# A hybrid language model's step: the second layer's recurrence from chunks of 32 to chunks of 64 tokens, with two preparations interleaved

## The chip, the core and the metric

The kernel runs on one core of a Trainium2 chip. TensorE (PE) multiplies, VectorE (DVE) and ScalarE (ACT) work on its results, GpSimd (POOL) does a few element-wise products and starts some DMAs, SyncE (SP) starts the weight loads. The metric is the device time of one execution in microseconds, the median of several runs.

## The reference

One forward step of a two-layer model with width 1024 over 512 prompt tokens and 8 decode sequences of 4 tokens (T = 544 columns). Layer 0 mixes tokens with two gated linear recurrences, layer 1 with the recurrence of RWKV-7; each is followed by a feed-forward part and a gated embedding part. The change is in layer 1's recurrence, which the reference runs token by token, for 16 heads of 64:

```python
def step(s, inp):
    r_t, lw_t, k_t, v_t, kk_t, a_t = inp
    s_kk = jnp.einsum('bhik,bhk->bhi', s, kk_t)
    s = (s * jnp.exp(lw_t)[:, :, None, :]
         - s_kk[..., :, None] * (kk_t * a_t)[..., None, :]
         + v_t[..., :, None] * k_t[..., None, :])
    return s, jnp.einsum('bhij,bhj->bhi', s, r_t)
```

The kernel computes it in chunks: within a chunk the tokens' mutual effect is a triangular system, whose inverse turns the removals and the values into updates; between chunks only the 64 x 64 state of each head is handed on.

## The kernel before, in words

All activations lie transposed, features on partitions and tokens on columns. Weights are split into an fp32r head and a rest (`w_head`, L293 on ACT; `w_rest`, L298 on DVE), and `unit_products` (L329) makes the dense products of all layers out of three fp32r products. `mixed` (L1742) and `dve_x` (L1751) make the inputs of layer 1's four projections r, k, g1 and v on DVE.

In layer 1, `dve_mix` scans the log decays per chunk (resets from `scan_resets(CO)`, CO = 32), `act_r` stores r, `act_k` and `dve_k` turn k, the decays and the removal keys into four scaled operands per feature tile: two key operands (`kb`, by chunk) and two query operands (`qrF`, `qr`). `wc` keeps the decay at each chunk's end.

The recurrence stands in `odd_late`. Four quads of 128 tokens and a fifth for the decode batch are prepared by `pe_prepare`, `act_prepare` and `dve_prepare`, which are generators: each `go_on(preparation, n)` lets an engine do the next n parts. The parts of a quad, in `parts_of`, are:

- sc: the key-query products of its 4 chunks (L2056), masked by DVE (L2159) and moved by ACT (L2133) and DVE (L2135),
- P and X for levels 2 to 5: the inverse is built by doubling. A level takes 128 P instructions (L2074), a copy by ACT (L2119), 128 X instructions (L2080), then on DVE a subtraction (L2179), a block transposition (L2197) and a masked product (L2198). Blocks are 32 x 32,
- vt and kt: transposes of values (L2066) and keys (L2069) to token rows, copied by ACT (L2111, L2115) or DVE (L2175).

A part's results go to one of PSUM banks 7, 0 and 1, and a part waits for the reader of its bank. A chunk n (`pe_chunk`, `act_chunks_odd`, `dve_chunks_odd`) has six streams of 16 products each on PE (32 instructions, since every fp32 product is two): av (L2217), R against the state (L2232), the state's part of the outputs oR (L2241), U through the inverse (L2247), and the two closing products, outputs (L2257) and new state (L2263). Between them stand ACT's copies of R (L2273) and half of U (L2277), DVE's other half of U (L2295), then DVE adds the state (h, L2303) and decays it (H, L2308), and ACT stores the outputs (L2285). The order on each engine is fixed: the quad's next parts are issued after R/oR (two), after U (one) and after the closing products (two). Each engine runs its own queue in order, so what stands in the queue behind a wait waits too.

The states of the decode sequences are loaded by GpSimd's DMA queue into two slots (`pool_states`, L2319), transposed by PE (L2086), stored by ACT (L2121) or DVE (L2184), and read for the decode tokens (L2094). `pool_masked_values` (L2353) makes masked values on GpSimd. `pe_late` (L2415) begins the gate part.

## Time and profile before

| | us |
|---|---|
| median of 3 runs | 2081.32 (2080.29 to 2083.05) |
| profiled execution | 2076.66 |
| its span | 2074.9 |
| PE busy | 1834.3 (88%) |
| DVE busy | 1026.3 (49%) |
| ACT busy | 720.8 (35%) |
| GpSimd busy | 128.7 (6%) |
| mean PE clock granted, share of full speed | 0.898 |

A row of a busy-time view has the stretch's start and end, its length, then for each engine the busy time and the number of instructions, then the PE clock as a share of full speed (0.50 is 1.2 GHz, 1.00 is 2.4 GHz), the DMA engines' mean share and GB/s. A timeline row has start, duration, engine, line, operation, output, input, shape and count, and in brackets the idle time before it and who ended it. A row of merged instructions lasts until the last one's modelled end, which overlaps the next row a little. In the chain of waits "issue" is time in which an engine waits for nothing that the profile shows. PEld is PE's weight load.

### The profile page before, as it was taken

How to read it: one execution, taken by the hardware profiler on the slowest of the kernel's cores; microseconds unless marked ns; L12 is line 12 of the kernel's file. 1: busy time of each engine (PE TensorE's matmuls, PEld its weight loads, DVE VectorE, ACT ScalarE, POOL GpSimd, SP SyncE). 2: the span in 40 equal slices, each digit the busy share in tenths (PEclk: the TensorE clock that was granted, in tenths of full speed). 3: DMA queues.
4: the chain of work that ended last, by engine and by line, in shares of the span. 5: the costliest groups of instructions: out<-in, count | busy, mean ns of one | idle time of the engine just before them, and what ended most of it. 6: DMA issues, size and time to landing. Idle time of an engine off the chain costs nothing.

```text
span 2074.9 us, 47908 instructions
## 1 busy us (share of the span) xinstructions
PE 1834.3 (88%) x21171; PEld 1708.4 (82%) x21171; DVE 1026.3 (49%) x1438; ACT 720.8 (35%) x923; POOL 128.7 (6%) x152
## 2 busy tenths in 40 slices
PE   4999977999999999957989767768889999999996
PEld 3999874999999999936868666657379999999996
DVE  5377766544334444566685433322464443444443
ACT  3353355254322224223453121211435451222333
POOL 1032450000000000000000000000100000000000
PEclk8999988999999999978999766665699999999998
DMA  3321131433322232211212100010024333233321
GB/s 100 81 72 52 52 103 29 112 113 91 101 72 81 81 105 69 72 42 31 82 54 71 33 4 4 4 23 25 0 65 124 88 91 94 61 91 91 92 72 43
DMA packets 237101, 138.61 MB, mean 67 GB/s; under 512 B 6560, under 2 KB 232160, under 8 KB 236944
## 3 DMA queue, kind: packets, MB, share of 16 engines
q1 hardware_dynamic: 226528, 114.31, 19.0%
q0 software_dynamic: 4048, 13.67, 2.7%
q10 hardware_dynamic: 6368, 8.24, 1.2%
q8 instruction: 135, 2.21, 0.4%
q14 instruction: 22, 0.18, 0.0%
HBM read 128.04 MB, written 8.16 MB: 66 GB/s over the span
## 4 chain that ended last, share of the span: by engine, by line
PE 76%; DVE 13%; ACT 4%; issue 4%; POOL 1%; DMA 1%; ACTq 0%; DVEq 0%; POOLq 0%
PE ps L329 59%; PE ps L2080 2%; PE ps L2074 1%; PE ps L1498 1%; DVE w_rest L298 1%; PE ps L1700 1%; ACT w_head L293 1%; PE ps L2232 1%; DVE x_split L1751 1%; PE ps L2241 1%; PE ps L2056 1%; POOL mix L855 1%; PE ps L964 1%; PE ps L2257 1%; PE ps L2217 1%
## 5 line engine op out<-in xcount | busy, mean ns | idle before, releaser
L329 PE MATMUL ps<-x_split,w_head 128*128 128x272 f32 (+1 forms) x5568 | 946.3, 293 | 51.5 <-DVE x_split L1751 20.8
L329 PEld LDWEIGHTS ps<-x_split,w_head 128*128 128x128 f32 x5568 | 801.5, 192 | 72.2 <-issue 48.4
L329 PE MATMUL ps<-x_split,w_rest 128*128 128x272 f32 (+1 forms) x2784 | 582.8, 291 | 0.0
L329 PEld LDWEIGHTS ps<-x_split,w_rest 128*128 128x128 f32 x2784 | 442.7, 192 | 0.0
L293 ACT ACTIVATE w_head<-w_raw 128x1024 fp32r<-128x1024 f32 (+1 forms) x206 | 228.3, 1108 | 605.5 <-PE ps L329 595.1
L298 DVE TENSOR_TENSOR w_rest<-w_raw,w_head 128x1024 fp32r<-128x1024 f32 (+1 forms) x206 | 268.3, 1303 | 193.2 <-ACT w_head L293 193.1
L329 PE MATMUL ps<-hidden_split,w_head 128*128 128x272 f32 x1408 | 233.2, 287 | 0.0
L329 PEld LDWEIGHTS ps<-hidden_split,w_head 128*128 128x128 f32 x1408 | 198.0, 188 | 0.0
L329 PE MATMUL ps<-hidden_split,w_rest 128*128 128x272 f32 x704 | 145.3, 287 | 0.0
L329 PEld LDWEIGHTS ps<-hidden_split,w_rest 128*128 128x128 f32 x704 | 110.1, 188 | 0.0
L1330 DVE TENSOR_TENSOR hT<-hT,ps 128x544 f32<-128x544 f32 (+1 forms) x40 | 28.8, 721 | 161.1 <-PE ps L329 161.1
L1462 DVE TENSOR_TENSOR mix<-mix,ps 128x544 f32<-128x544 f32 x44 | 31.7, 721 | 126.7 <-PE ps L329 126.7
L1458 DVE TENSOR_TENSOR mix<-mix,ps 128x544 f32<-128x544 f32 x44 | 31.7, 721 | 64.7 <-PE ps L329 58.7
L1448 ACT ACTIVATE hidden_split<-mix 128x544 f32 (+1 forms) x44 | 29.0, 659 | 91.3 <-DVE mix L1466 91.3
L1468 DVE TENSOR_TENSOR hidden_split<-mix,hidden_split 128x544 f32 (+1 forms) x44 | 31.9, 725 | 42.5 <-ACT hidden_split L1448 42.5
L2074 PE MATMUL ps<-odd_quad 32*32 32x32 f32 x2080 | 31.4, 227 | 16.2 <-issue 8.2
L2074 PEld LDWEIGHTS ps<-odd_quad 32*32 32x32 f32 x2080 | 28.5, 140 | 20.3 <-issue 10.6
L293 ACT ACT_TABLE_LOAD x21 | 26.9, 1283 | 52.1 <-PE ps L329 40.6
L964 PE MATMUL ps<-mix 64*64 64x64 f32 (+1 forms) x896 | 36.6, 229 | 8.1 <-DVE mix L882 8.1
L855 POOL TENSOR_TENSOR mix<-mix 128x256 f32<-128x256 f32 (+1 forms) x36 | 32.3, 897 | 158.5 <-DVE mix L882 88.6
L964 PEld LDWEIGHTS ps<-mix 64*64 64x64 f32 (+1 forms) x896 | 30.8, 140 | 11.6 <-DVE mix L882 9.2
L504 DVE TENSOR_TENSOR mix<-mix 128x544 f32<-128x544 f32 x48 | 34.5, 719 | 4.1 <-ACT mix L498 4.1
(390 smaller groups left out, 1993.3 us busy)
## 6 DMA issues: line engine op xcount, KB each, us to landing
w_raw<-in_w_ffn_gate SPq DMA_DIRECT2D x44, 512.0 KB, 3.8
w_raw<-in_w_ffn_up SPq DMA_DIRECT2D x44, 512.0 KB, 3.8
w_raw<-in_w_ffn_down SPq DMA_DIRECT2D x32, 704.0 KB, 4.6
w_raw<-in_w_in_even SPq DMA_DIRECT2D x29, 512.0 KB, 3.8
w_raw<-in_w_ple_gate SPq DMA_DIRECT2D x16, 512.0 KB, 4.0
w_raw<-in_w_out_even SPq DMA_DIRECT2D x8, 512.0 KB, 4.0
w_raw<-in_rw_wr SPq DMA_DIRECT2D x8, 512.0 KB, 4.1
w_raw<-in_rw_wk SPq DMA_DIRECT2D x8, 512.0 KB, 3.9
```

What stands on the lines that cost most here:

```text
L293: act.activation(wh[:, s, 0:kt * P], raw[:, s, 0:kt * P], ACT.Copy).then_inc(head_ok[s], 1)
L298: dve.tensor_tensor(wl[:, s, 0:kt * P], raw[:, s, 0:kt * P], wh[:, s, 0:kt * P].bitcast(F32), ALU.subtract).then_inc(rest_ok[s], 1)
L329: mm = pe.matmul(ps[:, 2 * s + h, 0:half.stop - half.start], w[:, s, k * P:(k + 1) * P], x[:, k, half], start=first and k == 0, stop=k == ...
L504: dve.tensor_tensor(n.sum, n.sum, n.sq[:, s, :], ALU.add).then_inc(sum_ok, 1)
L855: pool.tensor_tensor(e[:, :, 0, :], mid, b[:, :, 0, :], ALU.subtract)
L964: mm = pe.matmul(ps[64 * (c % 2):64 * (c % 2) + CE, b0 + level // 2, at:at + CE], left[:, c * CE:(c + 1) * CE], right[:, c * CE:(c + 1) * CE],
L1448: act.activation(hid[:, 0, ds(j, 1), :], prod.unsqueeze(1), ACT.Copy).then_inc(hhead_ok, 1)
L1458: dve.tensor_tensor(two(act_out), two(norm_f.rs), out2(0), ALU.mult).then_inc(bank_free[0], 1)
L1462: dve.tensor_tensor(two(prod), two(norm_f.rs), out2(1), ALU.mult).then_inc(bank_free[1], 1)
L1468: dve.tensor_tensor(hid[:, 1, ds(j, 1), :], prod.unsqueeze(1), hid[:, 0, ds(j, 1), :].bitcast(F32), ALU.subtract).then_inc(hrest_ok, 1)
L2074: mm = pe.matmul(at_block(out, p, g, j, i), at_block(bT, p, g, j, i), at_block(xx, p, g, j, i), start=True, stop=True)
L2080: mm = pe.matmul(at_block(out, p, g, j, i), at_block(pp, p, g, j, i), at_block(xTs[q % 2], p, g, j, i), start=True, stop=True)
```

## The change

The prompt's recurrence runs in 8 chunks of 64 tokens (CP) in place of 16 of 32; the decode batch keeps its blocks of 32.

- Scaling. Decays are still scanned per 32 tokens. `dve_r` now takes each chunk's sum over its first half (`half{t}`) and subtracts it from both log operands of that half (`mid{t}`), so that each 64-token chunk is scaled about its middle. `act_k` takes the exponent of these sums, `dve_k` multiplies them into the chunks' end decays (`decays`); the last key product and the copy of the first are each split into prompt and decode.
- Blocks. The 16 heads lie on the four 64 x 64 quarters of the array (`tile_heads`). A chunk has its own preparation stream m: aT (scores for the inverse), P and X for levels 2 to 6, A (scores for values), O (scores for outputs, 64 x 128 weights), vt, kt. X computes only the odd columns of a level, so 32 columns of 64. DVE subtracts half the width and transposes 32 x 32 blocks (`turned`); ACT copies half of the inverse to the other half of the partitions at each level (`other_rows`, two copies); the level masks are multiplied by GpSimd (`level_mask`) one level ahead.
- Order. Two streams are open at a time: stream n+1 (o in `in_chunk`) does its last 8 parts and stream n+2 its first 7 during chunk n. Before chunk 0 the first 7 parts of streams 0 and 1 alternate, then stream 0 is finished. Each stream has its own pair of PSUM banks (6 and 7, 0 and 1), and a part waits for the readers of its stream's part before.
- Chunk. U's weights are the 64 x 64 inverse; keys and values of both kinds lie on 128 rows, so the closing products have 128 x 64 weights. ACT's R copy, the U copies and the output copy are 512 columns per partition or as many as before per 64 tokens.
- The states' loads are started from the GpSimd stream; another table (`odd_levels`, 128 x 384 fp32) is loaded on ACT's queue; `g2` and the head spread, and the gate's split weights, lie elsewhere in memory; rw_r's products are cut into halves of 272 columns instead of 256 and 288, and `act_r` stores them with one copy.

The diff, cut to its core (the old functions stand above):

```diff
 CO = 32
-NCO = T // CO
+CP = 64
+NCP = TP // CP
+LEVELSP = 6
 GN_EPS = 64e-5
...
-    act.dma_start(tab[:, 0:1096], a["odd_tables"]).then_inc(*O0.dma.loaded("tab"))
+    act.dma_start(tab[:, 0:1064], a["odd_tables"]).then_inc(*O0.dma.loaded("tab"))
...
+        if t == 0:
+            dve.wait_ge(*O0.dve.at(f"a{KT - 1}"))
+        first = qrF[:, t, :, 0:TP].rearrange("p s (n h t) -> p s n h t", h=2, t=CO)[:, :, :, 0, :]
+        half = wc[:, t // 4, t % 4, 0:NCP]
+        dve.tensor_copy(half, first[:, 1, :, CO - 1]).then_inc(*O1.dve.done(f"half{t}"))
+        dve.wait_ge(*O1.dve.at(f"half{t}"))
+        dve.tensor_tensor(first, first, half.unsqueeze(1).unsqueeze(3).to_broadcast([P, 2, NCP, CO]),
+                          ALU.subtract).then_inc(*O1.dve.done(f"mid{t}"))
...
         act.activation(two(t1), out2(s), ACT.Copy, scale=col("rw_kk", t)).then_inc(*O1.act.done(f"k{t}"))
+        act.wait_ge(*O1.dve.at(f"mid{t if t else KT - 1}"))
+        if t == 0:
+            act.activation(wc[:, :, :, 0:NCP], wc[:, :, :, 0:NCP], ACT.Exp).then_inc(*O1.act.done("halves"))
         act.activation(e2, qrF[:, t, 1, :], ACT.Exp, scale=-1.0).then_inc(*O1.act.done(f"e2{t}"))
         act.activation(qrF[:, t, 1, :], qrF[:, t, 1, :], ACT.Exp)
         act.activation(qrF[:, t, 0, :], qrF[:, t, 0, :], ACT.Exp).then_inc(*O1.act.done(f"e{t}"))
         act.wait_ge(*O1.dve.at(f"be{t}"))
-        act.activation(keys_of(t)[:, :, 0, :], chunked(t2), ACT.Copy).then_inc(*O1.act.done(f"k0{t}"))
+        act.activation(keys_p(t, 0), by64(t2[:, 0:TP]), ACT.Copy)
+        act.activation(keys_s(t, 0), t2[:, TP:T], ACT.Copy).then_inc(*O1.act.done(f"k0{t}"))
 def act_v(act):
...
-        dve.tensor_tensor(chunked(grown), keys_of(t)[:, :, 1, :], chunked(grown), ALU.mult)
+        dve.tensor_tensor(grown, r_of(t), grown, ALU.mult)
         dve.wait_ge(*O1.dve.at(f"k0{t}"))
-        dve.tensor_tensor(chunked(e2), keys_of(t)[:, :, 0, :], chunked(e2), ALU.mult).then_inc(*O1.dve.done(f"be{t}"))
+        dve.tensor_tensor(e2, a_of(t), e2, ALU.mult).then_inc(*O1.dve.done(f"be{t}"))
         dve.tensor_tensor(qrF[:, t, 0, :], t1, qrF[:, t, 0, :], ALU.mult)
         dve.wait_ge(*O1.dve.at(f"be{t}"))
-        dve.tensor_tensor(keys_of(t)[:, :, 1, :], chunked(t1), chunked(e2), ALU.mult).then_inc(*O1.dve.done(f"end{t}"))
+        dve.tensor_tensor(keys_p(t, 1), by64(t1[:, 0:TP]), by64(e2[:, 0:TP]), ALU.mult)
+        dve.tensor_tensor(keys_s(t, 1), t1[:, TP:T], e2[:, TP:T], ALU.mult).then_inc(*O1.dve.done(f"end{t}"))
+    dve.wait_ge(*O1.act.at("halves"))
+    later = wc[:, :, :, NCP:2 * NCP - 1]
+    dve.tensor_tensor(later, later, wc[:, :, :, 1:NCP], ALU.mult).then_inc(*O1.dve.done("decays"))
     dve.wait_ge(*O1.pe.at(f"s{KT - 1}"))
...
+def parts_of(m):
+    if m == SAMPLE:
+        return [("sc", 0), ("P", 2), ("X", 2), ("vt", 0), ("kt", 0)] + [("st", b) for b in range(2, NB)] + [
+            ("rts", 0)]
+    parts = [("aT", 0)] + [(kind, level) for level in range(2, LEVELSP + 1) for kind in "PX"]
+    parts += [("A", 0), ("O", 0), ("vt", 0), ("kt", 0)]
+    return parts + [("st", 0), ("st", 1)] if m == SAMPLE - 2 else parts
+HEAD = 7
...
+def in_chunk(streams, n, slot):
+    order = ("o", "oo", "on", "nononononn")[slot]
+    for who in order:
+        if who == "o" and n + 1 in streams:
+            next(streams[n + 1], None)
+        if who == "n" and n + 2 in streams:
+            next(streams[n + 2], None)
+    if slot == 3:
+        for _ in streams.get(n + 1, ()):
+            pass
+def all_chunks(eng, stream, chunk):
+    streams = {m: stream(eng, m) for m in range(SAMPLE + 1)}
+    for _ in range(HEAD):
+        next(streams[0], None)
+        next(streams[1], None)
+    for _ in streams[0]:
+        pass
+    for n in range(SAMPLE + 1):
+        chunk(eng, n, lambda slot: in_chunk(streams, n, slot))
+def pe_stream(pe, m):
+    if m == 0:
         for s in range(2):
             pe.wait_ge(bank_free[s], used["rw_o"][s])
         pe.wait_ge(*O1.dve.at("nrm"))
...
+    par, before = m % 2, None if m < 2 else (m - 2, *parts_of(m - 2)[-1])
+    tokens = slice(CP * m, CP * m + CP) if m < SAMPLE else slice(TP, T)
+    for kind, x in parts_of(m):
+        if before is not None:
+            for by in readers(*before):
+                pe.wait_ge(*(O2.act if by == "act" else O2.dve).at(part_name(*before)))
+        bank = lambda b: ps[:, bank_of(m, b), :]
+        if m == SAMPLE and kind in ("sc", "P", "X", "vt", "kt", "rts"):
+            mm = pe_sample_part(pe, kind, bank)
+        elif kind == "aT":
+            for i, p, c in tile_heads:
+                mm = pe.matmul(bank(c)[half(1 - p), i * CP:(i + 1) * CP], keys_p(2 * i + p, 1)[half(c), m, :],
+                               qrF[half(c), 2 * i + p, 0, tokens], start=True, stop=True)
+        elif kind == "P":
+            pe.wait_ge(*O2.dve.at(f"t{m}_{x}"))
+            pe.wait_ge(*O2.pool.at(f"b{m}_{x}"))
+            for i, p, c in tile_heads:
+                mm = pe.matmul(bank(c)[half(1 - p ^ c), i * CP:(i + 1) * CP], bTs[par][x % 2][half(1 - p), head_cols(c, i)],
+                               xxs[par][half(1 - p), head_cols(c, i)], start=True, stop=True)
+        elif kind == "X":
+            pe.wait_ge(*O2.act.at(f"P{m}_{x}"))
+            for i, p, c in tile_heads:
...
+def other_rows(act, m, level):
+    act.wait_ge(*O2.dve.at(f"X{m}_{level}"))
+    for p in range(2):
+        mm = act.activation(xT2s[m % 2][half(p), :], xTs[m % 2][half(1 - p), 256:512], ACT.Copy)
+    mm.then_inc(*O2.act.done(f"x{m}_{level}"))
...
+def first_inverse(dve, m):
+    par = m % 2
+    n, width, lv, one = (8, CP, lvP, id64) if m < SAMPLE else (4, CO, lvS, id32)
+    view = lambda ap: ap[:, 0:n * width].rearrange("p (n t) -> p n t", t=width)
+    dve.tensor_tensor(view(bTs[par][1]), view(aTs[par]), lv[:, 0, :].unsqueeze(1).to_broadcast([P, n, width]),
+                      ALU.mult).then_inc(*O2.dve.done(f"b{m}_1"))
+    dve.wait_ge(*O2.dve.at(f"b{m}_1"))
+    dve.tensor_tensor(view(xTs[par]), one.unsqueeze(1).to_broadcast([P, n, width]), view(bTs[par][1]),
+                      ALU.subtract).then_inc(*O2.dve.done(f"X{m}_1"))
+    if m == SAMPLE:
+        dve.tensor_tensor(view(bTs[0][0]), view(aTs[0]), lvS[:, 1, :].unsqueeze(1).to_broadcast([P, n, width]), ALU.mult)
+    turned(dve, m, 2)
+def turned(dve, m, level):
+    w = 512 if m < SAMPLE else P
+    dve.wait_ge(*O2.dve.at(f"X{m}_{level - 1}"))
+    dve.transpose(xxs[m % 2][:, 0:w], xTs[m % 2][:, 0:w]).then_inc(*O2.dve.done(f"t{m}_{level}"))
...
+        elif m < SAMPLE and kind == "P" and x < LEVELSP:
+            if x == 2:
+                pool.wait_ge(*O2.dve.at(f"X{m}_1"))
+            else:
+                pool.wait_ge(*O2.pe.at(f"P{m}_{x - 1}"))
+            level_mask(pool, m, x + 1)
+        elif kind == "st" and x + 2 < NB:
+            pool.wait_ge(*O2.pe.at(part_name(m, kind, x)))
+            load_state(pool, x + 2)
+        yield
+def level_mask(pool, m, level):
+    view = lambda ap: ap.rearrange("p (n t) -> p n t", t=CP)
+    pool.tensor_tensor(view(bTs[m % 2][level % 2]), view(aTs[m % 2]),
+                       lvP[:, level - 1, :].unsqueeze(1).to_broadcast([P, 8, CP]), ALU.mult).then_inc(
+        *O2.pool.done(f"b{m}_{level}"))
+slot_in = [sem("state_in_even"), sem("state_in_odd")]
+slot_out = [sem("state_out_even"), sem("state_out_odd")]
+def load_state(pool, b):
+    pool.dma_start(lio[half(b % 2), :].rearrange("p (h k) -> p h k", h=HC),
...
+def pe_chunk(pe, n, go_on):
+    if n == SAMPLE:
+        pe_sample_chunk(pe)
+        return
+    par, tokens = n % 2, slice(CP * n, CP * n + CP)
+    vu, sA, sO, xT, xT2 = vus[par], sAs[par], sOs[par], xTs[par], xT2s[par]
+    pe.wait_ge(*O2.dve.at(f"A{n}_0"))
+    pe.wait_ge(*O2.dve.at(f"vt{n}_0"))
+    pe.wait_ge(*O2.act.at(f"vt{n}_0"))
+    for i, p, c in tile_heads:
+        mm = pe.matmul(ps[half(1 - p ^ c), 2 + c, i * NC:(i + 1) * NC], sA[half(p), head_cols(c, i)],
+                       vu[half(p), i, p, c ^ p, :], start=i == 0, stop=n == 0, skip_group_check=True)
     mm.then_inc(*O2.pe.done(f"av{n}" if n else "R0"))
...
+    go_on(0)
     if n > 0:
         pe.wait_ge(*O2.dve.at(f"H{n - 1}"))
         pe.wait_ge(*O2.pe.at(f"av{n}"))
...
+        for i, p, c in tile_heads:
+            mm = pe.matmul(ps[half(1 - p ^ c), 2 + c, i * NC:(i + 1) * NC], qrF[half(c), 2 * i + p, 0, tokens],
+                           hst[half(c), 2 * i + p, :], start=False, stop=True, skip_group_check=True)
         mm.then_inc(*O2.pe.done(f"R{n}"))
         pe.wait_ge(*O2.act.at(f"o{n - 1}"))
...
+        for i, p, c in tile_heads:
+            mm = pe.matmul(ps[half(c ^ p), 4 + p, 256 + i * CP:256 + (i + 1) * CP], hst[half(c), 2 * i + p, :],
+                           qrF[half(c), 2 * i + p, 1, tokens], start=i == 0, stop=False, skip_group_check=True)
         mm.then_inc(*O2.pe.done(f"oR{n}"))
...
+    go_on(1)
+    pe.wait_ge(*O2.act.at(f"R{n}"))
+    pe.wait_ge(*O2.dve.at(f"X{n}_{LEVELSP}"))
+    pe.wait_ge(*O2.act.at(f"x{n}_{LEVELSP}"))
+    for i, p, c in tile_heads:
+        o, g = 1 - p ^ c, c ^ p
+        inverse = xT2[half(o), i * CP:(i + 1) * CP] if c else xT[half(o), head_cols(c, i)]
+        mm = pe.matmul(ps[half(1 - p), 2 + g, 256 + i * NC:256 + (i + 1) * NC], inverse,
+                       rb[half(o), 256 * c + i * NC:256 * c + (i + 1) * NC], start=True, stop=True)
+    mm.then_inc(*O2.pe.done(f"U{n}"))
+    go_on(2)
+    pe.wait_ge(*O2.act.at(f"U{n}"))
+    pe.wait_ge(*O2.dve.at(f"U{n}"))
+    pe.wait_ge(*O2.dve.at(f"O{n}_0"))
+    pe.wait_ge(*O2.act.at(f"kt{n}_0"))
+    if n > 0:
+        pe.wait_ge(*O2.pe.at(f"oR{n}"))
+    for i, p, c in tile_heads:
+        g = c ^ p
+        pe.matmul(ps[half(g), 4 + p, 256 + i * CP:256 + (i + 1) * CP], vu[:, i, p, g, :],
+                  sO[:, 512 * c + (2 * i + p) * CP:512 * c + (2 * i + p + 1) * CP], start=n == 0 and i == 0, stop=True,
+                  skip_group_check=True)
+    for i, p, c in tile_heads:
+        at = P * n + 64 * c
+        mm = pe.matmul(ps[half(c), 4 + p, i * NC:(i + 1) * NC], rows_p[:, 2 * i + p, at:at + 64], vu[:, i, p, c ^ p, :],
...
+def act_chunk(act, n, go_on):
+    go_on(0)
+    act.wait_ge(*O2.pe.at(f"R{n}"))
+    if n < SAMPLE:
+        act.activation(rb.rearrange("p (c x) -> p c x", c=2), ps[:, 2:4, 0:256], ACT.Copy).then_inc(*O2.act.done(f"R{n}"))
+    else:
+        act.activation(rb[:, 0:256], ps[:, 2, 0:256], ACT.Copy).then_inc(*O2.act.done(f"R{n}"))
+    go_on(1)
+    act.wait_ge(*O2.pe.at(f"U{n}"))
+    dst = vus[n % 2][half(0), :, 1] if n < SAMPLE else vu_sample[32:64]
+    src = ps[half(0) if n < SAMPLE else slice(32, 64), 2:4, 256:512].rearrange("p g (i v) -> p g i v", i=4)
+    act.activation(dst.rearrange("p i g v -> p g i v"), src, ACT.Copy, scale=-1.0).then_inc(*O2.act.done(f"U{n}"))
+    go_on(2)
+    act.wait_ge(*O2.pe.at(f"o{n}"))
+    if n < SAMPLE:
+        act.wait_ge(*O2.dve.at(f"h{n}"))
+    tokens = slice(CP * n, CP * n + CP) if n < SAMPLE else slice(TP, T)
+    act.activation(qrF[:, :, 0, tokens].rearrange("p (i b) t -> p b i t", b=2), out_sum(n), ACT.Copy).then_inc(
+        *O2.act.done(f"o{n}"))
+    go_on(3)
```

## Rows read from the trace of the kernel before

**Rows 1.** busy time by stretch of the stage: length, each engine's busy us (instructions), PE clock, DMA

```profile
1156.96:1197.60 40.64, 26.49 (x1184) 22.59 (x1184) 14.46 (x25) 7.23 (x12) 0.00 (x0) 0.63 0.07 15
...
1197.60:1389.30 191.70, 138.26 (x5792) 120.21 (x5792) 65.77 (x101) 37.31 (x72) 0.00 (x0) 0.65 0.02 4
...
1389.30:1454.05 64.75, 49.65 (x1366) 43.72 (x1365) 15.68 (x29) 11.18 (x25) 7.49 (x10) 0.50 0.15 36
```

**Rows 2.** chain of waits, 1197.6 to 1389.3 us: its shares, and one of its pieces

```profile
by line: issue 19.4%; PE ps L2080 12.4%; PE ps L2074 11.8%; PE ps L2232 6.0%; PE ps L2241 5.6%; PE ps L2056 5.5%; PE ps L2217 4.8%; PE ps L2066 4.3%; DVE odd_quad L2159 4.1%; PE ps L2247 3.8%; PE ps L2257 3.7%; PE ps L2263 3.6%; DVE odd_qua
...
1222.01 1.87 issue
```

**Rows 3.** DMA of the same stretch, all queues: packets, bytes, sizes

```profile
DMA packets 46, 0.75 MB, mean 4 GB/s; under 512 B 0, under 2 KB 0, under 8 KB 0
```

**Rows 4.** the largest group by line and shape, same stretch: busy us, mean ns, idle

```profile
L2074 PE MATMUL ps<-odd_quad 32*32 32x32 f32 x1536 | 23.7, 227 | 9.0 <-issue 8.2 <-DVE odd_quad L2198 0.5
```

**Rows 5.** timeline at PE clock 0.50: start, us, engine, line, shape, count

```profile
1246.24 1.08 PE L2232 MATMUL ps<-mix 64*32 64x64 f32 x32 [0.18 <-PE ps L2217]
...
1247.25 1.08 PE L2241 MATMUL ps<-mix 64*64 64x32 f32 x32
...
1251.34 1.11 PE L2069 MATMUL ps<-ident,mix 128*128 128x128 f32 x4
...
1251.45 0.69 DVE L2179 TENSOR_TENSOR mix<-mix,ps 128x512 f32<-128x512 f32 x1 [9.69 <-PE ps L2080]
```

**Rows 6.** timeline of a state's transposes at PE clock 0.50, and what they wait for

```profile
1415.12 1.63 POOL L2319 DMA_DIRECT2D mix<-in_state_rwkv  x2 [16.48 <-PE ps L2086]
...
1419.30 1.08 PE L2086 MATMUL ps<-ident,mix 64*128 64x64 f32 x8 [3.09 <-DMA mix<-in_state_rwkv]
```

**Rows 7.** timelines at PE clock 1.00: three shapes of products

```profile
1271.27 1.16 PE L2056 MATMUL ps<-mix 64*64 64x64 f32 x64
...
1272.25 0.62 PE L2257 MATMUL ps<-odd_quad,mix 64*64 64x32 f32 x32
...
245.87 0.69 PE L964 MATMUL ps<-mix 128*64 128x64 f32 x16
...
298.89 1.90 PE L1032 MATMUL ps<-mix 64*128 64x64 f32 x32
```

**Rows 8.** timeline of one level of a preparation that runs alone

```profile
1177.10 1.93 PE L2074 MATMUL ps<-odd_quad 32*32 32x32 f32 x128 [1.61 <-DVE odd_quad L2198]
...
1179.09 0.60 ACT L2119 ACTIVATE odd_quad<-ps 128x512 f32<-128x512 f32 x1 [2.96 <-PE ps L2074]
...
1180.01 2.00 PE L2080 MATMUL ps<-odd_quad 32*32 32x32 f32 x128
...
1182.77 0.71 DVE L2197 STREAM_TRANSPOSE odd_quad<-odd_quad 128x512 f32<-128x512 f32 x1
...
1184.20 1.28 PE L2074 MATMUL ps<-odd_quad 32*32 32x32 f32 x128 [1.15 <-DVE odd_quad L2198]
```

**Rows 9.** the masked values' products on GpSimd: ns min/median/max

```profile
L2353 POOL TENSOR_TENSOR odd_quad<-odd_quad,tables x8: 1031/1038/1491, 1452.5 to 1482.1; 128x512 f32<-128x512 f32 x8
```

**Rows 10.** timeline of the last chunks, which carry no preparation

```profile
1440.17 1.08 PE L2232 MATMUL ps<-mix 64*32 64x64 f32 x32 [0.52 <-DVE mix L2308]
...
1447.68 1.08 PE L2232 MATMUL ps<-ident,mix 64*32 64x64 f32 x32 [0.57 <-DVE mix L2308]
```

**Rows 11.** busy time of PE in four stretches: length, busy us (instructions), clock, DMA

```profile
1265.00:1268.40 3.40, 3.40 (x125) 0.50 0.02 5
...
1268.40:1275.00 6.60, 5.08 (x201) 0.98 0.01 2
...
1424.60:1431.40 6.80, 6.80 (x256) 0.50 0.02 5
```

**Rows 12.** DVE around the step from the first to the second projection

```profile
1001.64 1.23 DVE L298 TENSOR_TENSOR w_rest<-w_raw,w_head 128x1024 fp32r<-128x1024 f32 x1 [4.76 <-ACT w_head L293]
...
1016.73 1.23 DVE L298 TENSOR_TENSOR w_rest<-w_raw,w_head 128x1024 fp32r<-128x1024 f32 x1 [1.46 <-ACT w_head L293]
```

More of the change, by code:

```diff
@@ L2181, in dve_prepare @@
[L2181 to L2190 removed]
+                        s = 1 << (x - 1)
```

655 lines of the change are left out of this document (313 added, 342 removed).

## The prediction

> **What bounds the kernel now.** I first read busy time by stretch. The second layer's recurrence takes 297.1 us, from the first score product to the first product of the gate part, in three parts: the first quad's preparation alone (40.6 us), twelve chunks of 32 tokens with preparations between their steps (191.7 us, so 32.0 us per 64 tokens), and the last four chunks with the decode batch (64.8 us) [rows 1]. No engine is full: in the middle part PE is busy for 72% at a clock of 0.65, DVE for 34%, ACT for 19%. The chain of waits says where the rest goes: 19.4% is "issue", in gaps such as 1.87 us where PE waits for nothing that the profile shows [rows 2]. That is 37.2 us, or 6.2 us per 64 tokens. The DMA view of that stretch holds 46 packets and 0.75 MB [rows 3], 16 KB each; over its 5792 pairs of a product and a weight load that is 65 bytes an instruction. I take it that nothing but instructions is moved, one packet per 126 pairs. I read the gaps as PE having run through its instructions before the next packet: they come in the streams of 32x32 blocks (1536 instructions, 9.0 us of idle time before them, 8.2 of it issue [rows 4]), which use up a pair in 15 ns (128 in 1.93 us [rows 8]).
>
> The Trainium skill's page "Runtime: NRT & Kernel Launch", section "Instruction fetch mechanics", has the same 16 KiB blocks, but calls the cost of crossing into one mostly hidden. By it the gaps would not shrink with the instruction count, which is the slower rival below; here they cost 0.8 us a packet, so I go by the trace.
>
> **Instruction count.** A fp32 product is two pairs. Before, 64 tokens take 976 pairs: 592 of preparation (a quad of 128 tokens: 128 score, 8 x 128 inverse, 32 transposes) and 2 chunks x 192. After, preparation takes 32 each for aT, A, O and ten inverse steps (416), 4 + 8 transposes, and the chunk 4 x 32 + 64: 620 pairs, 36% fewer, each covering more of the array.
>
> **Prices on PE.** At clock 0.50, 32 pairs of 64x64 blocks with 64 or 32 columns take 1.05 and 1.01 us: the 32x64 stream starts at 1246.24 and the next at 1247.25, and 1.08 with the tail is the same for both forms [rows 5]. At clock 1.00, 64 pairs take 0.98 us to the next start [rows 7]; I use 0.55 per 32. Four transposes take 1.04 us slow, half of that fast. The closing products become 128x64 weights: 16 pairs take 0.69 us with their tail of 0.07 at clock 1.00 [rows 7], so 32 take 1.25 fast and, at the ratio of the 64x64 form, 2.3 slow, twice per chunk. O has 64x128 weights: 32 pairs took 1.74 us to the next start at clock 1.00 [rows 7], and 8 transposes of that shape took 1.08 at 0.50 [rows 6]. So slow O lies between 1.7 us (clock of no account) and 4.3 (all in series); I take 3.4, twice the fast row, nearest to it in form. The skill's page "TensorE: Matmul & The Clock Gate", section "LDWEIGHTS", lets a load's time follow its columns and not its rows. By it alone the closing products would cost no more than 64x64 ones, 2.5 us less per chunk at the slow clock and some 10 us less over six chunks; the row shows 39 ns a pair against 15, so I stay with the row.
>
> PE's work per 64 tokens is then 11 x 1.05 + 5 x 1.01 + 3.4 + 3.1 + 4.6 = 27.7 us slow and 14.9 fast. Before it is 26.2 slow: the change leaves PE's time alone and takes gaps and waits.
>
> **Prices elsewhere.** ACT copies 128x512 in 0.60 us, DVE transposes it in 0.71 [rows 8] and subtracts in 0.69 [rows 5]; the halved subtraction I take at 0.4. The level masks move to GpSimd, 1.03 us each [rows 9], five per chunk, always a step ahead: nothing, and 0.3 us a level if they came late. New on ACT are two 64-row copies per level, 0.8 us together (estimate: two 256-column copies).
>
> **One chunk n walked through at the slow clock** (us from its start, in PE's order; (+1), (+2) are the two preparations). av 0; P5(+1) 1.3, after DVE; R 2.35; oR 3.4; X5 4.45; P6 6.8, after a wait of 1.3 for DVE's subtraction and transposition; U 7.85; X6 8.9; aT(+2) 9.95; closing products 11.0 to 15.6; P2(+2); A(+1) 16.65; X2 18.8, a wait of 1.1, since ACT must first store the outputs after DVE's h, then do its row copies and P2; O 19.85 to 23.25; P3; vt 24.85, 0.55 behind DVE's two masks of O; X3 25.9; kt 26.95; P4 to 30.1; X4 at 31.9, a wait of 1.8 for ACT (kt's copy of 1.05, row copies, P4). Next chunk at 33.0. H is done before its reader comes, so the recurrence itself is off the path; R copies and U copies hide behind P6, X6 and aT. At the fast clock the same walk gives 23, with 8 us of waits. With 30% of the time fast, as now (0.65 [rows 1]), 1/(0.3/23 + 0.7/33) = 29.2; I add 0.3 for gaps that are left, since 128 pairs last 4.2 us slow but 2.2 us fast: **29.5 us** per 64 tokens against 32.0.
>
> **The stage's sum.** Start, by the same walk: score products and first inverse until 4.1, three levels of both streams until 18.6, two levels of the first alone until 26.8, then A, O, vt and kt with their copies in series until 37.8, against 40.6; before, one level alone is 7.1 us [rows 8]. Six full chunks: 177. Two states' transposes with their copies: 3. Chunk 6, whose (+2) is the small decode batch with two states: 28. Chunk 7: 25, with states 4 to 7 (their loads take some 4 us, waits of 3.1 [rows 6]; two stand in the open) and 7 us of decode reads; then the decode chunk, 8 as now (a bare chunk is 7.5 [rows 10]). Sum 278.8, against 297.1: -18.3.
>
> **Outside the stage.** The eight shifts about the middle add 8 x (a 0.17 copy + 0.7) on DVE during the first projection. Seven lie in its idle time (4.76 us before one weight split [rows 12]); that of unit 6 stands ahead of the next projection's inputs, on the path: +0.9. That of unit 7 fits into 1.46 us of idle [rows 12]. The split end product adds 0.1 on DVE per unit of the second projection: +0.2 on the path. The extra table load (196 KB) comes early: 0, or 2 at worst. Sum -17.2.
>
> The profiled execution took 2076.7 us, 4.6 under the median of 2081.3: 2059.5 in its terms, **2064 against the median**. Below 0.2%, about 4.2 us, a measurement cannot tell a change from none.
>
> **Rivals.**
> (1) The gaps stay (0.15). They would belong to each stretch of time and not to each instruction: 6.2 us per 64 tokens again. In place, six chunks: +35 at the most, 2064 + 35 = 2099; if they shrink with the pairs only (3.9 us), +22, 2086. It decides from 3 us of gaps per chunk. For it: the trace shows gaps and packets side by side, not that one makes the other. Against: the bare chunk [rows 10], whose pairs take 33 ns, needs 7.5 us with 6.2 of products and 1.3 for its handovers: no gap is left in it.
> (2) The clock stays at its lower level (0.12, together with (4)): 33.0 per chunk, +21, 2085, no change. Both happen now: 6.8 us of unbroken 64x64 products with 8 columns stayed at 0.50; an unbroken stretch of R, oR and score products was followed by 0.98 [rows 11]. In the walk P6 to A is 10 us with hardly a break, so I expect rises, but every level has waits that can end them.
> (3) Denser than walked (0.18): PE has fewer breaks, so the fast level holds for some three quarters of the time, 1/(0.75/23 + 0.25/33) = 25 per chunk: -27 more, 2037. For it speaks that the longest unbroken runs of PE grow.
> (4) The interleaving does not do what it says: both streams use ACT, in one fixed order, and a chunk's output copy stands before P2's. If each of the 12 handovers cost 0.3 more than walked, a chunk is 33 us, as in (2), and the price is the same.
> The forecast keeps 0.55, from 2050 to 2078. Faster: 0.55 + 0.18 and a little of the others' lower halves, 0.74; within 0.2%: 0.11; slower: 0.15. For 8 in 10 the range takes in (3) and the lower end of (1), and O's bounds (-10 to +5 over six chunks): 2036 to 2088.
>
> **What would show it.** In the profile after: the stage near 279 us; some 4960 pairs in it, and the stretch's packets down to 29 in six chunks; issue under 1 us per 64 tokens; chunks 29 to 30 us apart; PE at 0.6 to 0.7; O between 1.7 and 3.4; waits for DVE before P6 and for ACT before X2 and X4; GpSimd never waited for; the start near 38 us; 1 us more before the second projection. Wrong it would be if issue stays over 3 us a chunk, if the clock reads 0.5 or over 0.8 throughout, or if a wait that I put at nothing (GpSimd's masks, H, U's copies) stands among the longest.

## The result and the profile after

The changed kernel takes 2047.18 us (median of 4 runs, 2047.12 to 2057.42) beside 2080.81 for the one before (4 runs): a ratio of 0.9853, interval [0.9819, 0.9887], some 31 us. The forecast was 2064, 17 us faster, within 2036 to 2088: the sign and most of the mechanism held, the size was about half of what was measured. The profiled executions are 2076.66 and 2047.15 us, 29.5 apart. One run of the kernel with the keys' copy on DVE (below) took 5873.56 us and is left out everywhere.

Busy time of the changed kernel by stretch of the stage, in the columns of [rows 1]: the start until the first av, six chunks, chunk 6, and chunk 7 with the decode batch.

```profile
1157.49:1197.44 39.95, 24.62 (x656) 21.75 (x659) 18.78 (x30) 14.03 (x29) 13.38 (x11) 0.59 0.07 15
1197.44:1371.24 173.80, 126.44 (x3676) 114.72 (x3679) 75.81 (x114) 73.52 (x142) 42.17 (x30) 0.74 0.01 3
1371.24:1392.88 21.64, 16.90 (x541) 15.15 (x541) 9.40 (x20) 8.72 (x17) 2.95 (x3) 0.94 0.11 27
1392.88:1424.05 31.17, 22.21 (x642) 20.26 (x641) 5.60 (x9) 4.38 (x9) 5.07 (x7) 0.57 0.19 55
```

The stage is 266.6 us where it was 297.1: 30.5 less, all of the gain. Of it 0.7 us lie in the start, 17.9 in the six chunks and 11.9 in the last part (52.8 where it was 64.8, which ran at clock 0.50 before [rows 1]). Outside, the stage begins 0.5 us later, and what follows it is 0.3 us shorter, which is no difference.

| part | forecast | measured | difference |
|---|---|---|---|
| start | 37.8 | 39.95 | +2.15 |
| six chunks with two states | 180 | 173.8 | -6.2 |
| chunk 6 | 28 | 21.6 | -6.4 |
| chunk 7 and decode batch | 33 | 31.2 | -1.8 |
| stage | 278.8 | 266.6 | -12.2 |

The six chunks in the chain of waits, its shares by line:

```profile
by line: PE ps L2109 13.9%; PE ps L2117 11.3%; ACT mix L2206 8.1%; PE ps L2125 6.5%; PE ps L2103 6.2%; issue 4.6%; ACT odd_quad L2206 4.5%; DVE odd_quad L2303 4.5%; PE ps L2122 3.8%; DVE mix L2249 3.7%; DVE odd_quad L2249 3.3%; ACT mix L221
```

In the DMA view of the six chunks, the instruction queue's packets, MB and share of the DMA engines' time, before and after:

```profile
q8 instruction: 45, 0.74, 1.6%
...
q8 instruction: 29, 0.48, 1.1%
```

By line and shape, the groups of GpSimd's masks, of O and of the first inverse, in the columns of [rows 4]:

```profile
L2335 POOL TENSOR_TENSOR mix<-mix,odd_levels_on_chip 128x512 f32<-128x512 f32 x15 | 21.3, 1420 | 82.5 <-ACT mix L2206 51.1 <-PE ps L2103 29.6 <-DVE mix L2240 1.9
...
L2117 PE MATMUL ps<-mix 64*128 64x64 f32 x192 | 20.0, 390 | 0.0
...
L2240 DVE TENSOR_TENSOR mix<-mix 128x512 f32<-128x512 f32 x3 | 4.9, 1647 | 0.1
```

Issue has gone from 19.4% of 191.7 us [rows 2] to 4.6% of 173.8, which is 37.2 to 8.0 us, and packets of the instruction queue from 45 (of the 46 of [rows 3]) to 29. PE's busy time went only from 138.3 to 126.4 us. The chain counts every engine's short pauses as issue. PE's own idle time that waits for nobody is the clearer measure of the gaps: 34.8 us in the twelve old chunks, in seven groups, and 3.2 in the six new ones, in three. From the view of waits, engine and line, whom it waited for, us in total, times, longest; the two largest before and the three after:

```profile
PE ps L2080 <- issue: 9.9, 9, 1.7
PE ps L2074 <- issue: 8.2, 8, 2.1
...
PE ps L2103 <- issue: 1.5, 2, 1.1
PE ps L2097 <- issue: 1.2, 1, 1.2
PE ps L2391 <- issue: 0.5, 1, 0.5
```

So the gaps gave back 31.6 us and PE's busy time 11.8, while PE's waits for other work rose from 18.6 us to 44.2: together the 17.9 us of the stretch. The costliest step of the chain beside X is now O (L2117), 3.3 us a chunk; next to it stand the copies of ACT (L2206) that the X parts (L2109) wait for.

One chunk of the changed kernel, PE's timeline from one av (1253.91) to the next (1283.81), without the rows between:

```profile
1260.12 0.64 PE L2103 MATMUL ps<-odd_quad 64*64 64x64 f32 x29 [1.64 <-DVE odd_quad L2249]
...
1263.96 0.21 PE L2097 MATMUL ps<-mix 64*64 64x64 f32 x1 [1.20 <-issue]
1264.19 1.81 PE L2391 MATMUL ps<-odd_quad 128*64 128x64 f32 x32
1265.74 1.98 PE L2396 MATMUL ps<-odd_quad,mix 128*64 128x64 f32 x32
1268.06 0.69 PE L2103 MATMUL ps<-mix 64*64 64x64 f32 x32 [0.35 <-issue]
...
1270.85 0.79 PE L2109 MATMUL ps<-mix 64*64 64x32 f32 x32 [1.63 <-ACT mix L2206]
1271.57 3.68 PE L2117 MATMUL ps<-mix 64*128 64x64 f32 x32
...
1276.64 1.11 PE L2122 MATMUL ps<-ident,mix 128*128 128x128 f32 x4 [0.33 <-DVE odd_quad L2303]
...
1283.35 0.67 PE L2109 MATMUL ps<-mix 64*64 64x32 f32 x32 [1.68 <-ACT mix L2206]
```

The walk of the prediction is there in its order, with waits where it put them: 1.64 before P6 (1.3 walked), 1.63 before X2 (1.1), 0.33 before vt (0.55), 1.68 before X4 (1.8). The closing products take 3.5 us from their start to their end (4.6 walked), and a gap of 1.20 us stands in the middle of aT, at clock 1.00.

What lay between the subtraction of the first inverse (L2240) and X2 in that chunk, from the chain of waits:

```profile
1264.84 0.70 DVE mix L2237
1265.56 1.66 DVE mix L2240
1267.25 0.71 DVE mix L2249
1267.96 0.58 DVE mix L2469
1268.62 0.60 ACT mix L2453
1269.24 0.41 ACT mix L2217
1269.67 0.41 ACT mix L2217
1270.11 0.60 ACT mix L2206
1270.85 0.79 PE ps L2109 x32
```

L2240 takes 1.66 us; the kernel before has the same subtraction (L2171), and it took 0.69 there. DVE's sum of the state (L2469) stands behind it, ACT's output copy (L2453) waits for that sum, and P2's copies stand behind the output copy. No step of the prediction had this delay.

### The profile page after: what moved, and what is told of

Read it like the earlier page. It is cut to its first block, busy times and chain, and to the rows that moved or that the text cites. A ratio compares the mean times of both kernels' runs of the same rounds, so it can differ in the third digit from the quotient of the medians.

```text
span 2044.6 us, 42447 instructions
## 1 busy us (share of the span) xinstructions
PE 1811.9 (89%) x18335; PEld 1694.2 (83%) x18335; DVE 1042.3 (51%) x1481; ACT 765.7 (37%) x1012; POOL 184.3 (9%) x192
## 3 DMA queue, kind: packets, MB, share of 16 engines
q8 instruction: 113, 1.85, 0.4%
## 4 chain that ended last, share of the span: by engine, by line
PE 75%; DVE 14%; ACT 6%; issue 3%; POOL 1%; DMA 1%; ACTq 0%; DVEq 0%; POOLq 0%
PE ps L340 59%; PE ps L2109 1%; PE ps L2117 1%; PE ps L1509 1%; PE ps L2103 1%; DVE w_rest L309 1%; PE ps L1715 1%; ACT w_head L304 1%; ACT mix L2206 1%; DVE x_split L1766 1%; PE ps L2125 1%; PE ps L1051 1%; POOL mix L866 1%; PE ps L975 1%; DVE mix L540 1%
## 5 line engine op out<-in xcount | busy, mean ns | idle before, releaser
L1341 DVE TENSOR_TENSOR hT<-hT,ps 128x544 f32<-128x544 f32 (+1 forms) x40 | 28.8, 721 | 161.3 <-PE ps L340 161.3
L2206 ACT ACTIVATE mix<-ps 128x512 f32<-128x512 f32 (+2 forms) x39 | 26.3, 676 | 64.5 <-PE ps L2103 20.9
```

What stands on the lines that cost most here:

```text
L1341: dve.tensor_tensor(h, h, out2(s), ALU.add).then_inc(bank_free[s], 1)
L2206: act.activation(dst, src, ACT.Copy).then_inc(*O2.act.done(name))
```

## Experiments

All ratios are against the kernel before, run on the same chip. They ran on three chips, where the kernel before took 2079.2 us (one preparation at a time, mask, O, keys' copy), 2075.4 (bare stream, the first filling of breaks, three and four edits) and 2076.1 (the rest). "Stage" is measured in the profiled execution, from the first aT to the first gate product. One profile has its own scatter: behind its bare stream, the kernel with 1024 pairs is the changed one, and there the stage took 268.4 us beside 266.6, the six chunks 173.1 at clock 0.72 beside 173.8 at 0.74. So differences of some 2 us in a stage say nothing.

### One preparation at a time

```diff
-        HEAD = 7
+        HEAD = 0
...
-            order = ("o", "oo", "on", "nononononn")[slot]
+            order = ("oo", "oooo", "ooo", "oooooo")[slot]
```

> The changed kernel with its preparations one after the other: chunk n does all parts of stream n+1, and before chunk 0 only stream 0 is prepared. Blocks, instructions and scaling are as in the changed kernel. Theory: interleaving is what hides the handovers between PE, ACT and DVE. A level alone takes about 4.2 us (two products, ACT's copy, DVE's subtraction and transposition in series), five of them 21, with aT and the first inverse, A, O, vt and kt about 37 us, of which the chunk's own products hide little: chunks some 38 us apart in place of 29, less about 10 us saved before chunk 0: about 2100 us. Rival: the gain came from the smaller number of instructions alone, and the handovers hide behind the chunk's products either way: within 6 us of the changed kernel's 2047.

Measured: 2148.84 us, ratio 1.0336 [1.0306, 1.0367]. The six chunks, in the columns of [rows 1], and three rows of PE's timeline:

```profile
1191.73:1439.05 247.32, 152.71 (x3674) 138.41 (x3673) 76.41 (x114) 73.25 (x140) 41.92 (x31) 0.60 0.01 2
```

```profile
1254.05 1.97 PE L2391 MATMUL ps<-odd_quad 128*64 128x64 f32 x32
1255.81 1.92 PE L2396 MATMUL ps<-odd_quad,mix 128*64 128x64 f32 x32
1257.66 0.86 PE L2103 MATMUL ps<-mix 64*64 64x64 f32 x32
```

Chunks are 40.5 us apart in place of 28.4, the stage is 368.9 us, and the kernel is slower than the one with 32-token chunks. The theory holds and its 2100 us was too low: the new blocks, prepared one chunk after the other, lose 70 us against the kernel before, the interleaving brings 102 back. The clock is 0.60 where it was 0.74, with the same products: PE stands idle for 94.6 us of the six chunks in place of 47.4. The timeline also gives the closing products at clock 0.50: 1.76 and 1.85 us from start to start, where the prediction scaled 2.3 each.

### 1024 pairs of 32x32 on PE alone

```diff
+                for k in range(512):
+                    r = c = 32 * (k % 4)
+                    pe.matmul(ps[c:c + 32, 6, 0:32], ident[r:r + 32, c:c + 32], ident[r:r + 32, 0:32], start=True, stop=True)
```

> The changed kernel with 512 more fp32 products of 32x32 blocks (1024 pairs of a product and a weight load) on PE alone, unbroken, just before the first score product. Theory: a block of 256 instructions (128 pairs) is supplied at the soonest some 3.6 us after the block before it was entered; the eight blocks then take 8 x 3.6 = 29 us, with a gap of about 1.7 us after every 128 pairs. Rival 1: every crossing costs the same 0.8 us: 1024 x 15 ns + 8 x 0.8 = 22 us. Rival 2: the gaps belong to time or to other engines' work and not to instructions: 15.4 us without gaps.

The timeline of PE (one execution, 2079.56 us in all):

```profile
1157.51 3.21 PE L2088 MATMUL ps<-ident 32*32 32x32 f32 x223 [3.47 <-DVE mix L1982]
1161.88 1.93 PE L2088 MATMUL ps<-ident 32*32 32x32 f32 x128 [1.17 <-issue]
1165.34 1.93 PE L2088 MATMUL ps<-ident 32*32 32x32 f32 x128 [1.53 <-issue]
1169.07 1.93 PE L2088 MATMUL ps<-ident 32*32 32x32 f32 x128 [1.80 <-issue]
...
1180.56 1.93 PE L2088 MATMUL ps<-ident 32*32 32x32 f32 x128 [2.08 <-issue]
```

A gap after every 128 pairs, in a stream that waits for nobody. In the 27.7 us the DMA view has 7 packets of the instruction queue, 16 KB each, which is 256 instructions or 128 pairs at 64 bytes:

```profile
q8 instruction: 7, 0.11, 1.6%
```

So the gaps are the instruction supply. It gives 128 pairs in 3.46 to 4.01 us (mean of six, to the start of the last 33 pairs at 1184.57, 3.78), 29.5 ns a pair, while the products need 15. The whole stream took 27.7 us, as the supply theory has it (29); a fixed 0.8 us per crossing (22) and gaps that belong to time (15.4) are out. So a gap is what a block lacks to 3.8 us: 1.9 us after 32x32 blocks, some 1.6 after fast 64x64 ones, nothing after slow ones, whose 128 pairs last 4.2. Before, 976 pairs per 64 tokens needed 28.8 us of supply in a period of 32.0; now 620 need 18.3 in 28.4.

### GpSimd's mask a step later

```diff
                 if m < SAMPLE and kind == "aT":
-                    pool.wait_ge(*O2.act.at(part_name(m, kind, x)))
+                    pool.wait_ge(*O2.dve.at(f"X{m}_1"))
                     level_mask(pool, m, 2)
```

> The changed kernel, with GpSimd's mask of level 2 started after DVE's first inverse and not beside it. Theory: DVE's subtraction of two operands in SBUF (1.65 us in the trace, 0.69 in the kernel before) waits while GpSimd works on its mask. With the mask later it takes 0.7 us, the mask comes about 0.35 us after the transposition, so the wait before P2 falls by some 0.6 us per chunk: 2 to 5 us faster, 2043 to 2045. Rival: this form of the subtraction is slow by itself; then it stays at 1.65, P2 waits longer for the mask, and the time is 2047 to 2050.

Measured: 2032.01 us, ratio 0.9785 [0.9759, 0.9811]; the stage is 255.9 us, 10.7 less than in the changed kernel, the clock of the six chunks 0.75. Groups of the six chunks:

```profile
L2117 PE MATMUL ps<-mix 64*128 64x64 f32 x192 | 14.0, 303 | 0.0
...
L2103 PE MATMUL ps<-mix 64*64 64x64 f32 x480 | 14.4, 279 | 9.6 <-DVE mix L2249 6.5 <-POOL mix L2335 3.1
...
L2474 DVE TENSOR_TENSOR mix<-mix,w_raw 128x512 f32<-128x512 f32 x6 | 10.2, 1692 | 0.2
...
L2240 DVE TENSOR_TENSOR mix<-mix 128x512 f32<-128x512 f32 x3 | 2.1, 692 | 0.1
```

The subtraction is back at 0.69 us, and the delay sits on the next product of two SBUF operands that meets a mask, H (L2474, 0.69 before the edit, 1.69 now), which nobody waits for. The theory holds, but 10.7 us of the stage came where it had 2 to 5. (The median is 15 us lower; 5.8 us of the profile's difference lie ahead of the stage, where the code is the same.) Of the 10.3 us that the six chunks lost, 4.2 are waits before X parts (23.3 to 19.1), 0.4 waits before P parts (18.0 to 17.6, of which 5.3 now wait for GpSimd's mask, as the theory had it), and 6.0 are O, 3.3 us before and 2.3 now: same instructions, at a higher clock more often.

The Trainium skill's page "SBUF — State Buffer", section "SBUF: two separate sides", says that a DVE operation with two SBUF inputs and a GpSimd operation that reads SBUF share a port pair, an "exclusive lock", and that the second fully blocks until the first is done. The trace agrees: 0.69 + 0.96 us for the DVE operation that came behind the start of GpSimd's mask, nothing for the one that came ahead of it (L2237, 0.70).

### O in two halves

```diff
-                    for i, p, c in tile_heads:
-                        mm = pe.matmul(bank(c)[:, (2 * i + p) * CP:(2 * i + p + 1) * CP], rows_p[half(c), 2 * i + p, P * m:P * m + P],
+                    for i in range(4):
+                        for q, p, c in ((q, p, c) for q in range(2) for p in range(2) for c in range(2)):
+                            h = p ^ q
+                            mm = pe.matmul(bank(c)[half(h), (2 * i + p) * CP:(2 * i + p + 1) * CP],
+                                           rows_p[half(c), 2 * i + p, P * m + 64 * h:P * m + 64 * h + 64],
...
```

Each head has one product for each half of its 128 weight columns, and four products in a row lie on four quarters.

> The changed kernel with O's products cut into two 64-token halves, so that its 32 pairs with 64x128 weights become 64 pairs with 64x64 ones on the four quarters. Theory: O is dear (3.6 us at the low clock, 2.0 at the high one) since a weight of 128 columns takes both column halves and only two such products run side by side; 64 pairs at the 64x64 rate are 2.1 and 1.0 us, O stands on the chain, so each chunk is 1.0 to 1.5 us shorter: 2036 to 2040. Rival: PE is supplied with instructions at some 28 ns a pair; then 64 pairs need at least 1.8 us and the 32 more per chunk bring new gaps: 2043 to 2048.

Measured: 2031.77 us, ratio 0.9781 [0.9757, 0.9806]; the stage is 250.9 us, 15.7 less, the clock 0.79. The group of O in the six chunks:

```profile
L2119 PE MATMUL ps<-mix 64*64 64x64 f32 x384 | 8.7, 251 | 0.0
```

O costs 1.45 us where it was 3.3. That is 11.3 of the 13.0 us of the six chunks, and the issue share rose from 4.6 to 5.3% only: the theory holds, and the median is beyond it. Its rival, new gaps from 32 more pairs per chunk, is worth 1.5 us (PE idle for nobody, 3.2 to 4.7).

### The keys' copy on DVE

```diff
+            if kind == "kt" and m < SAMPLE:
+                return ("dve",)
...
```

> The changed kernel with the copy of the transposed keys (128x1024, 1.02 us on ACT) moved from ACT to DVE. Theory: this copy stands in ACT's queue ahead of the row copies and of P4's copy, and the wait before X4 (1.63 us, for ACT) falls by 1.0 to 1.6 us in each of six chunks, nothing else being late: 2038 to 2042. Rival: DVE is next in line: its copy (about 1.4 us) delays the subtraction after X4 and the wait moves to P5: 2045 to 2049.

Measured: 2039.73 us (median of five), ratio 0.9819 [0.9792, 0.9846]; the intervals overlap with the changed kernel's. By the profiles the stage is 6.0 us shorter and every chunk about 27.5 us. The median lies in the theory's range and the stage's gain at its lower end (1.0 us a chunk); by the times alone it isn't told from none.

### Breaks in PE's work filled

Three transposes of a constant stand ahead of each X part.

```diff
                 elif kind == "X":
+                    for _ in range(3):
+                        pe.transpose(bank(1)[:, 256:384], ident[:, :], ident[:, :])
                     pe.wait_ge(*O2.act.at(f"P{m}_{x}"))
```

> The changed kernel with three more transposes of a constant (128x128, 0.26 us each at the low clock, 0.13 at the high one) ahead of each X part, where PE waits 0.8 to 1.6 us for ACT's copy. Theory: the waits are what drops the clock; with them filled the clock granted in the six chunks rises from 0.74 to 0.85 or more, and what follows (O above all, 3.6 us low, 2.0 high) gets cheaper by more than the transposes cost where the wait was shorter: 2030 to 2044. Rival: the clock does not follow PE's business at this scale and stays near 0.74; the transposes cost what does not fit the waits: 2050 to 2065.

Measured: 2064.91 us, ratio 0.9954 [0.9936, 0.9972]. The design failed: every part first waits for the reader of the part before, which for X is the same copy, so the transposes ran behind the wait and filled nothing (clock 0.76, six chunks 185.6 us). The second try put them ahead of the P parts' wait for DVE's transposition:

> The changed kernel with three more transposes of a constant ahead of each P part, placed so that they run while PE would wait for DVE's transposition (0.71 us of a wait of 1.3 to 1.6); the earlier run had them behind the wait, and so they filled nothing. Theory: breaks in PE's work are what takes the clock down; with them partly filled the clock of the six chunks rises from 0.74 to over 0.80, and the chunks stay at 29 us or fall to 27, since what the transposes cost (0.4 us where the wait was already covered) comes back: 2035 to 2050. Rival: the clock stays near 0.74; the transposes then cost time wherever the wait is shorter than they are: 2050 to 2060.

Measured: 2043.15 us, ratio 0.9833 [0.9812, 0.9854], and in the six chunks:

```profile
1192.70:1363.28 170.58, 134.48 (x3764) 116.95 (x3763) 75.80 (x114) 73.45 (x142) 42.50 (x30) 0.80 0.01 3
```

```profile
L2101 PE MATMUL ps<-ident 128*128 128x128 f32 x90 | 20.4, 346 | 3.4 <-DVE mix L2294 1.6 <-DVE odd_quad L2294 1.6
```

PE does 20 us of work that nobody needs, and the six chunks together are 3.2 us shorter, at a clock of 0.80 in place of 0.74 (0.72 in the second profile of the same code). The theory holds at its lower edge: when breaks are filled, the granted clock is higher, and it paid for the filling. It is no gain in itself (start and tail gave it back, the stage is 267.3).

### Four edits together, and a delay put on purpose

The kernel with the mask, O and copy edits together; then with a fourth edit, ACT's output copy behind the copies for P2 and X2 (`act_chunk` does the parts "non" before the copy and "onononn" after it).

> The changed kernel with all three edits: the mask of level 2 later on GpSimd, O in two halves, the keys' copy on DVE. Theory: they shorten different waits, and the gains in the stage (10.7, 15.7 and 6.0 us by the profiles) add up but for what mask and O share (each makes O cheap): some 24 us, 2020 to 2026. Rival: they all buy the same clock, and together give no more than the best of them: 2030.

> The same, and ACT stores a chunk's outputs after the copies that P2 and X2 wait for and not before them. Theory: the output copy waits for DVE's sum of the state and then takes 0.6 us in front of P2's copies; without it the wait before X2 (1.0 us) is shorter by 0.6 to 0.9 us per chunk: 4 to 6 us less than the run with three edits. Rival: the outputs are then late for the products of the next chunk or another ACT copy moves in their place: no difference.

Measured: 2019.54 us, ratio 0.9719 [0.9692, 0.9747], stage 237.5; and 2013.01 us, 0.9698 [0.9666, 0.9730], stage 231.2, clock 0.90. Three edits save 29.0 us of the stage, where their gains by themselves add up to 32.4: they add, less a tenth, which is more than the theory's 24, and its rival is out. The fourth is 6.3 us by the profiles and 6.5 by the medians, a little above the theory's 4 to 6; by the intervals it isn't settled.

```diff
             dve.wait_ge(*O2.dve.at(f"b{m}_1"))
+            if m < SAMPLE:
+                dve.tensor_tensor(view(xxs[par]), one.unsqueeze(1).to_broadcast([P, n, width]), view(bTs[par][1]),
+                                  ALU.subtract)
```

> The kernel with four edits, and DVE does each first inverse's subtraction twice (once into a tile that is overwritten), so that 0.69 us is put on the path before every P2. Theory: a wait costs its own length and then more, since the clock falls behind it: over eight streams well over 8 x 0.69 = 5.5 us, 9 to 16 us more than without it (2013), with the clock in the six chunks down from 0.90. Rival: a wait costs what it lasts: 4 to 6 us more, the clock unchanged.

Measured: 2022.88 us, ratio 0.9751 [0.9736, 0.9767]. By the medians the delay costs 9.9 us (11 by the ratios, which allow for the other chip; their intervals do not overlap), as the theory has it; by the profiles the stage is 6.7 us longer, near the rival's 4 to 6, and the six chunks 4.2, six times 0.7, at 0.88. The profiled execution (2017.6) was the fastest of the five, and the one that it is compared with (2015.4) the slowest but one. Whether a wait costs more than itself at this clock stays open.

### aT ahead of P6

The kernel with four edits, and PE and ACT do aT of stream n+2 in the slot before U; DVE's first inverse stays behind U.

```diff
-            order = ("o", "oo", "on", "nononononn", "non", "onononn")[slot]
+            order = ("o", "ono" if early else "oo", "o" if early else "on", "nononononn", "non", "onononn")[slot]
...
```

> The kernel with four edits, and PE and ACT do the scores aT of stream n+2 before P6 of stream n+1 and not after X6. Theory: PE waits 1.35 us for DVE before P6 with nothing to do; aT's 0.5 us fits there, and the first inverse, which DVE does after U, finds aT ready, so that P2 waits less: 0.5 to 0.9 us per chunk, 3 to 5 us less than 2013. Rival: U's copies lose their cover (aT stood behind U and X6), and the closing products wait instead: no difference, or 2 us more.

Measured: 2009.38 us, ratio 0.9681 [0.9661, 0.9701]; the stage is 227.0 us. The six chunks:

```profile
1194.19:1329.96 135.77, 99.39 (x3865) 88.11 (x3864) 83.23 (x121) 65.20 (x133) 39.97 (x30) 0.91 0.02 4
```

Its median is 3.6 us under the kernel with four edits and the stage 4.2, as the theory has it; the intervals overlap. It is the fastest kernel of the study and beats the changed one by some 36 us (0.9681 against 0.9853). Its PE works 73% of the time, as in the changed kernel, but at 0.91. Nor is it the sum of PE's idle time that differs from the kernel with the filled waits: 36.4 us of these six chunks and 36.1 of those, which ran at 0.80.

## Why the prediction was right, and where its size was off

**Gaps, right.** The first step, that the gaps are instruction supply and go with the pairs, was shown by the bare stream. Packets came to 29 as forecast. "Issue under 1 us per 64 tokens" holds for PE, whose gaps are 0.5 us a chunk (3.2 in six); by the chain's issue, which is what the prediction read before, it was too low, 1.3 us (8.0 in six). Rival (1) put 3.9 or 6.2. The stage's trace has 5515 pairs: the forecast's 4960 are the prompt's (8 x 620) and leave out the decode batch's.

**The rule of the page, against the trace.** The bare stream executes 128 pairs in 1.93 us and is supplied with them in 3.78. The Trainium skill's page "Runtime: NRT & Kernel Launch", section "Instruction fetch mechanics", calls the crossing of a 16 KiB block mostly hidden, since dispatching is slower than filling. The trace disagrees for these small products. The prediction's 0.8 us a packet was a mean over blocks with gaps and without.

**Walk, right in kind.** 27.7, 28.9, 29.9, 28.5 and 27.0 us for five chunks, a mean of 28.4 against 29.5, with every large wait at its place. O took 3.6 us at clock 0.50 and 1.9 at 1.00 to the next start (3.4 and 1.74 walked). The fast sum of PE's work comes to 14.6 us by the prediction's own prices, not 14.9; no other number hangs on it.

**The step that failed: "with 30% of the time fast, as now".** The clock share was carried over from the kernel before. A mean clock of 0.74 is 48% of the time fast. With 48% the prediction's own formula gives 1/(0.48/23 + 0.52/33) = 27.3, and with PE's gaps of 0.5 us 27.8, or 28.6 with the chain's 1.3, beside 28.4 measured: the mixture was wrong. The fit is partly luck, since two errors inside the walks, of about 1 us a chunk each, cancel: the closing products' price and the wait that GpSimd causes (both below). "So I expect rises" stood in rival (2) and was priced in rival (3), and should have moved the forecast itself; rival (3)'s 25 us a chunk did not come, and X parts still waited 23.3 us for ACT in the six chunks. The single chunks go with their clock: 28.9, 29.9, 28.5 and 27.0 us at 0.76, 0.71, 0.76 and 0.81. That breaks bear on the clock is shown by the filled waits (0.80 against 0.72 and 0.74, one profile each); which breaks count stays open, for the fastest kernel has as much idle time as the filled one, at 0.91.

**Chunk 6, over-priced: half of the 12.2 us.** It was put at 28 us without a shown walk and took 21.6 at clock 0.94. The clock is the smaller part of it: the kernel with the bare stream has the same code there, and chunk 6 took 23.4 us at 0.74.

```profile
1398.84:1422.26 23.42, 19.97 (x541) 18.34 (x541) 9.41 (x20) 8.72 (x17) 2.96 (x3) 0.74 0.10 25
```

So some 4.6 of the 6.4 us are there at the clock of the full chunks. With the decode batch's small parts in place of a stream's, it has 541 pairs where a full chunk has 620, and PE stood idle for 3.5 us, where a full chunk of the changed kernel has 7.9. In the other kernels with two streams it took 21.3 to 23.7 us, and 25.6 with the filled waits.

**Closing products, over-priced.** 2.3 us each at the slow clock was a ratio borrowed from the 64x64 form; 1.76 and 1.85 were measured, and 1.0 (kernel with four edits) against 1.25 at the fast one. That is some 1 us a chunk. They take 55 to 58 ns a pair at clock 0.50 against 33 for 64x64. The Trainium skill's page "TensorE: Matmul & The Clock Gate", section "LDWEIGHTS", lets a load's time follow its columns, and for a single load the trace agrees. In the kernel with one preparation at a time, at clock 0.50 (duration in ns, least, median and most):

```profile
L2396 PEld LDWEIGHTS ps<-odd_quad,mix x32: 227/227/227, 1255.7 to 1257.3; 128*64 128x64 f32 x32
```

There a 64x64 load (L2113) took 223 ns at the same clock, and in the changed kernel one of 64x128 took 330; at clock 1.00 the three are 138, 135 and 188. What differs, by these figures, is how many pairs overlap: at 0.50 a 128x64 load lasts some 4 times the time between two pairs, a 64x64 one 6.8 times. The prediction's step from one load's time to "no more than 64x64 ones" left that out; the row that it went by instead had it, and only its scaling to the slow clock was off.

**GpSimd, wrong.** "Always a step ahead: nothing" looked for a late mask. The masks never were late (no P part waited for one), but the first of each stream held DVE's subtraction for 0.96 us, and through it h, the output copy and X2. The start shows it as well, where DVE's first two operations took 1.78 and 1.63 us: with level 2's mask later it was 38.7 us, with three edits (O's cheaper form among them) 37.2, beside 39.95 in the changed kernel and 37.8 forecast. Its own price was off too: 1.27 us alone, not 1.03 [rows 9]. This term, put at nothing, costs some 1 us a chunk by itself; it hid behind the over-priced closing products and the better clock. Taken away, it gave back 10.7 us.

**Outside the stage.** Forecast +1.1, measured +0.5 before it and -0.3 after it. The table load cost nothing that can be seen.

**Rival (4)** had it that the interleaving might do nothing. Without it the kernel is 102 us slower: the new blocks do not pay without it. The rival's price of +0.3 us per handover did not appear: the large waits of the chunk shown came within 0.6 us of the walk.

## What to carry to other kernels

Count instructions where products are small: here a pair of a product and a weight load must last 30 ns on average, or PE waits for its instructions. In the six chunks the gaps are most of what the larger blocks gave (34.8 to 3.2 us). Larger blocks here also mean more levels in series, each with its handovers between engines: five per 64 tokens, where four served 128. So they paid only with a second, independent stream between the handovers. When the clock is between its levels, don't carry its share over from the kernel before: a wait taken away ahead of a long step can give back more than its length (six times 0.96 us held DVE, and the six chunks became 10.3 us shorter), and a GpSimd product beside DVE's two-operand ones may cost DVE what it was meant to save.
